# A decoder step on one core: two alternating buffers for the shared expert, and raw x turned with the norm's factors at the evictions

## The reference

```
h  = rmsnorm(x) * norm_mix_g;  z = h @ w_in          # q, k, v, o (512 each), gates i, f (4 each), u (512)
mix = [ mLSTM heads(q, k, v, i, f) * head_norm_g * sigmoid(o) | pooled(u) @ w_pool * pool_scale ]
x  = x + mix @ w_out
x  = x + shared_expert(rmsnorm(x)) + sum over top-8 of 64 experts: gate_e * (silu(h@w1_e) * (h@w3_e)) @ w2_e
x  = x + (p @ w_ple) * sigmoid(rmsnorm(x) @ w_gate);  y = rmsnorm(x) * final_norm_g
```

## Time and profile before

| | us |
|---|---|
| median of 3 runs | 1052.86 (1051.55 to 1054.36) |
| the profiled execution | 1053.18 |
| its span, first to last instruction | 1051.4 |
| start, until the gates (L1924) | 0 to 18.9 |
| projections, mixer, router, shared expert | 18.9 to 366 |
| expert loop | 366 to 956 |
| tail | 956 to 1051 |
| busy: PE, DVE, POOL, ACT | 985.3, 448.5, 360.4, 156.2 |

### The profile page before, as it was taken

The page is one execution under the profiler, slowest core; times in us unless marked ns, Lnnn a source line. Parts: engine busy times, 40 slices in busy tenths (PEclk is TensorE's granted clock), DMA queues, the critical chain, the costliest instruction groups (busy, mean ns, idle before and its releaser), DMA issues.

```text
span 1051.4 us, 16052 instructions
## 1 busy us (share of the span) xinstructions
PE 985.3 (94%) x5686; PEld 447.1 (43%) x5686; DVE 448.5 (43%) x1287; ACT 156.2 (15%) x383; POOL 360.4 (34%) x434
## 2 busy tenths in 40 slices
PE   5999999989999999999899899899899898999996
PEld 4777655645544433333233233233233233333443
DVE  4201222345549754344334344344333434452885
ACT  3110023301021101001011010001001001002322
POOL 5000321211024444444344344354344444451232
PEclk9999999999999999999999899899999999999999
DMA  9032223122149599999999999999999999796942
GB/s 295 20 92 80 81 78 90 54 67 70 41 147 386 192 371 400 413 413 413 411 396 413 405 394 412 403 390 413 390 394 402 387 402 397 283 366 257 422 159 80
DMA packets 76307, 296.43 MB, mean 282 GB/s; under 512 B 16250, under 2 KB 26682, under 8 KB 49381
## 3 DMA queue, kind: packets, MB, share of 16 engines
q1 hardware_dynamic: 59693, 258.14, 63.3%
q0 software_dynamic: 16576, 37.80, 9.4%
HBM read 277.08 MB, written 32.54 MB: 294 GB/s over the span
## 4 chain that ended last, share of the span: by engine, by line
PE 71%; DMA 14%; DVE 6%; issue 4%; POOL 2%; DVEq 1%; ACT 1%; SPq 0%; POOLq 0%; ACTq 0%
PE bank L1900 22%; PE bank L2270 19%; DMA xT<-in_ex_w 9%; PE bank L2249 6%; PE bank L2334 5%; PE bank L2252 5%; DMA arena<-xs_dram,slot 5%; PE bank L2273 4%; PE bank L1906 1%; POOL arena L919 1%; PE bank L1986 1%; PE bank L1996 1%; PE bank L2283 1%; PE bank L2033 1%; DVE arena L1816 1%
## 5 line engine op out<-in xcount | busy, mean ns | idle before, releaser
L2270 PE MATMUL bank<-arena 128*32 128x512 f32 x1536 | 240.3, 624 | 32.3 <-DMA xT<-in_ex_w 18.9
L919 POOL DMA_INDIRECT arena<-xs_dram,slot x200 | 220.8, 1104 | 71.1 <-issue 63.2
L2270 PE MATMUL bank<-xT,arena 128*32 128x512 f32 x512 | 239.8, 624 | 0.0
L2270 PEld LDWEIGHTS bank<-arena 128*32 128x32 f32 x1536 | 65.4, 114 | 179.8 <-issue 172.4
L934 POOL DMA_INDIRECT y_dram<-arena,outrow x48 | 49.1, 1024 | 267.7 <-DVE slot L1702 225.4
L2249 PE MATMUL bank<-arena 128*32 128x512 f32 x640 | 116.2, 595 | 0.8 <-ACT arena L1143 0.8
L1716 DVE STREAM_TRANSPOSE arena<-arena 128x1024 f32<-128x1024 f32 x50 | 62.2, 1243 | 86.7 <-DMA arena<-xs_dram,slot 86.7
L1900 PE MATMUL bank<-xT,ring 128*128 128x288 f32 x384 | 93.4, 406 | 0.0
L1900 PEld LDWEIGHTS bank<-xT,ring 128*128 128x128 f32 x384 | 72.9, 190 | 20.5 <-issue 0.5
L1139 ACT ACTIVATE arena<-bank 128x256 f32<-128x256 f32 x48 | 18.5, 385 | 358.9 <-PE bank L2270 253.0
L1764 DVE COPY outrow<-yrow 128x1 int32<-128x1 int32 x48 | 7.4, 154 | 144.2 <-PE bank L2249 94.5
(11 more groups left out here) (402 smaller groups left out, 1244.9 us busy)
## 6 DMA issues: line engine op xcount, KB each, us to landing
arena<-in_ex_w SPq DMA_DIRECT2D x96, 1024.0 KB, 15.2
ring<-in_ex_w SPq DMA_DIRECT2D x40, 1024.0 KB, 15.9
xT<-in_ex_w SPq DMA_DIRECT2D x32, 1024.0 KB, 10.4
arena<-y_dram SPq DMA_DIRECT2D x18, 1024.0 KB, 10.9
mixpj<-in_ex_w SPq DMA_DIRECT2D x16, 1024.0 KB, 12.3
ring<-in_w_in SPq DMA_DIRECT2D x5, 2048.0 KB, 8.3
wide<-in_ex_w SPq DMA_DIRECT2D x8, 1024.0 KB, 18.5
ring<-in_w_out SPq DMA_DIRECT2D x2, 2048.0 KB, 8.8
```

The lines of the kernel that those rows point to most:

```text
L919: pool.indirect_dma_start(xg[b][:, 256 * a:256 * a + 256], None, xs_quarter, bass.IndirectOffsetOnAxis(slot[k][:, a:a + 1], 0), bounds_che ...
L2270: ins = pe.matmul(bank[2][t, :], xgT[b][:, c, t], w13[k if lane < 3 else 3][:, :, wc, :], start=(c == 0), stop=(c == KT - 1))
```

## The change

Two edits in one. In the loop, own(j) becomes j % 3 and fourth(j) = 3 + j // 3 % 2 is new: the shared expert alternates between slots 3 and 4 and is loaded two periods ahead, the three own slots are refilled each period. SP's order and PE's waits follow. The last loads of SP are reordered: gt1, gt0, and then g_b, which now waits for the last w2 matmuls.

At the start PE turns x as it came. norm_mix_g is loaded with one value per partition and 128-row piece (g1) and multiplied in at the evictions of the turned tiles, all on DVE. POOL makes diag(rstd) for each tile; five matmuls of ones with it give rB, rstd along the free axis on all partitions, which ACT brings to SBUF. q and k (now evicted by DVE), u and the gates are multiplied by rB at their eviction, v and o by rstd as a value per partition (o's tanh takes rhalf = rstd / 2 as its scale). The gate biases are added after that, in two more passes.

```
-        g += [(("x1T", i, 0), "v"), (("x1T", i, 1), "s")]
-    g += [(("g",), "v")]
-    g += [(("q", j, n), "s") for j in range(H) for n in range(2)]
-    g += [(("k", j, n), "s") for j in range(H) for n in range(2)]
+        g += [(("x1T", i, 0), "v"), (("x1T", i, 1), "v")]
+    g += [(("rB", 0), "s"), (("rB", 1), "s"), (("g",), "v")]
+    g += [(("q", j, n), "v") for j in range(H) for n in range(2)]
+    g += [(("k", j, n), "v") for j in range(H) for n in range(2)]
...
-            return j % 3 or j // 3 % 2 * 4
+            return j % 3
+        def fourth(j):
+            return 3 + j // 3 % 2
...
-            sp.dma_start(g_a[:, :], bc(norm_mix_g[0])).then_inc(s_ga, 16)
+            sp.dma_start(g1, norm_mix_g[0].rearrange("(c p) -> p c", p=P),
+                         allow_slow_non_contiguous=True).then_inc(s_ga, 16)
...
-            e = expert(4)
+            e = expert(7)
...
+            def period(done, slot_c, place, last=None, more_c=True):
+                e = expert(place(0))
+                sp.wait_ge(s_mm1, done + 1)
+                load13(0, e)
                 if last is not None:
                     f = expert(last)
                     sp.wait_ge(s_mm2, done)
-                    load2(2, f)
+                    load2(7 - slot_c, f)
+                f, e = e, expert(place(1))
                 sp.wait_ge(s_mm1, done + 2)
                 load13(1, e)
+                sp.wait_ge(s_mm2, done + 1)
+                load2(0, f)
                 f, e = e, expert(place(2))
                 sp.wait_ge(s_mm1, done + 3)
                 load13(2, e)
+                sp.wait_ge(s_mm2, done + 2)
+                load2(1, f)
+                f = e
+                if more_c:
+                    e = expert(place(7))
+                    sp.wait_ge(s_mm1, done + 3)
+                    load13(slot_c, e)
                 sp.wait_ge(s_mm2, done + 3)
-                load2(3, f)
+                load2(2, f)
...
+            sp.wait_ge(s_mm1, more * STEPS + (STEPS - 2))
             load_chunk("gt1")
-            sp.wait_ge(s_mm2, more * STEPS + (STEPS - 2))
-            sp.dma_start(g_b[:, :], bc(final_norm_g)).then_inc(s_gb, 16)
             sp.wait_ge(s_mm2, more * STEPS + (STEPS - 1))
             load_chunk("gt0")
+            sp.wait_ge(s_mm2, more * STEPS + STEPS)
+            sp.dma_start(g_b[:, :], bc(final_norm_g)).then_inc(s_gb, 16)
...
             for i in range(NT):
+                r = ROWS[i]
                 rms(i, 0)
+                pool.wait_ge(s_rstd, i + 1)
+                pool.tensor_scalar(diag[0:r, i, 0:r], ident[0:r, 0:r], rstd[0:r, i:i + 1], None, ALU.mult
+                                   ).then_inc(s_diag, 1)
...
+            for i in range(NT):
+                r = ROWS[i]
+                for n in range(2):
+                    b = full_bank(dve, "x1T", i, n)
+                    drain("v", dve.tensor_tensor(
+                        xT[:, 4 * n:4 * n + 4, tok(i)], b[:, :].rearrange("p (c t) -> p c t", t=P)[:, :, 0:r],
+                        g1[:, 4 * n:4 * n + 4].unsqueeze(2).to_broadcast([P, 4, r]), ALU.mult), "x1T", i, n)
+
+            wait_drained(dve, "rB", 1)
+            dve.wait_ge(s_rstd, NT)
             b = full_bank(dve, "g")
...
+            for name, dst, scale in (("q", qT, float(P) ** -0.5), ("k", kT, 1.0)):
+                for j in range(H):
+                    for n in range(2):
+                        c = slice(TH * n, TH * n + TH)
+                        b = full_bank(dve, name, j, n)
+                        drain("v", dve.scalar_tensor_tensor(out=dst[:, j, c], in0=b[:, 0:TH], scalar=scale, in1=rB[:, c],
+                                                            op0=ALU.mult, op1=ALU.mult), name, j, n)
...
             for i in range(NT):
-                pe.wait_ge(s_xs, i + 1)
-                turn("x1T", i, xs1[:, i % 2, :])
+                pe.wait_ge(s_x[i], 16)
+                turn("x1T", i, x[:, i, :])
+            for n, tiles in enumerate((range(NP_), (NP_,))):
+                b = free_bank(pe, "rB", n)
+                for k, i in enumerate(tiles):
+                    r = ROWS[i]
+                    pe.wait_ge(s_diag, i + 1)
+                    ins = pe.matmul(b[:, P * k:P * k + r], onesf[0:r, :], diag[0:r, i, 0:r], start=True, stop=True)
+                ins.then_inc(filled, 1)
```

## The result

The changed kernel takes 1047.06 us (median of 5 runs, 1045.96 to 1048.96) against 1052.86: ratio 0.9944, interval 0.9930 to 0.9958. It is faster by 5.8 us, where 18.4 were forecast. The profiled execution has a span of 1047.2 us and a time of 1048.96.

The account below looks back on a forecast made before the run. The prediction took PE and DMA as both near full, the loop bound by DMA with stalls on the single shared buffer; 15.7 + 3.0 - 0.3 = 18.4 us off 1053.2 gave 1034.8, range 1028 to 1048.

Parts of the forecast that it names:

- The start: Before the gate matmuls: raw x turned, shorter path through rstd, gates begin at 15.9 instead of 18.91, 3.0 us gained.
- The tail: After the last w2 matmuls: g_b's load moved ahead of the y8 loads, taken as 0.3 us lost.
- term of 15.7 us: Expert loop, 420 to 930 us: its 202.2 MB at 409 GB/s take 494.3 us instead of 510, 15.7 gained.
- so this wait goes: Expert loop: two alternating shared buffers end PE's wait for the shared w1/w3 load, up to 19.1 us against a 15.3 gap.
- mean of 409 GB/s: Expert loop, 420 to 930 us: mean DMA rate taken to rise from 396.4 to 409 GB/s.
- 26.5 us, against up to 24.1 us to landing: Own experts' loads, the tightest left: freed at step j, wanted at j+3, 26.5 us later; landing takes up to 24.1.
- the wait only moves: Loop rival, 22%: stalls form on own experts' loads, the mean stays 399 GB/s, 6.3 us gained, 1047 us.
- 12.2 us a step from 12 to 42: Expert loop, sign to look for in the profile after: steps 12 to 42 at 12.2 us each, where before had 12.56.
- The slower rival: Loop rival, 8%: a deeper weight queue makes gathers land 1 us later, 12.8 us lost, 3.0 gained, 1063 us.
- the two bounds set: Gather pieces in the chain: under 9 us expected by the forecast; above 10 the slower rival holds.
- The 16 us: Loop gathers: called the slower rival's cost, to be 0 if DMA engines serve queue rows in turn.
- the second rival: Loop rival, 22%: the wait moves to own experts' loads; 3.3 us gained there plus 3.0 at the start, 1047 us.

Follow-up runs that it names:

- e_start: Start of the change alone (raw x turned, factors at the evictions), with the loop and tail of the kernel before: 1049.34 us, ratio to before 0.9960 to 0.9986.
- e_gb: Changed kernel with g_b's load issued behind the y8 loads and DVE's wait moved to its first use: 1045.91 us.
- e_order: Changed kernel with slot 0's next w1/w3 load issued by SP ahead of the previous period's slot 2 w2 load: 1044.49 us.
- e_bhalf: Kernel before, with only the first half of each w2 loaded and used twice: 1033.38 us.
- e_late: Changed kernel with SP's order and g_b's load mended (1042.5 us), plus the shared w1/w3 load issued one step later, behind slot 0's next: 1045.55 us.
- e_buffers: Buffers and tail of the change alone, with the start of the kernel before: 1049.97 us, ratio to before 0.9962 to 0.9987.

## Why the prediction was wrong, point by point

**The start** had the right path and about the right size, with some luck: 3.0 us forecast. In ten profiles with the new start the loop's first matmuls begin at 362.4 us on average, in three with the old one at 365.6, so 3.2. Only 2.5 of them are at the gates, where the path of the forecast ends: they begin at 16.25 on average for 18.77. The other 0.7 are the clock. From the gates to the loop it takes 346.8 to 347.0 us in six of the ten, with a granted clock of 0.83 from 210 to 220 us, and 345.1 to 345.3 in the four others, with 1.00; the three old ones, each with one such fall, took 346.8 to 347.0. Whether the change spares the fall in those four isn't shown. These are the windows of the changed kernel and of e_start, columns as in the earlier trace rows:

```profile
210.00:220.00 10.00, 7.98 (x32) 4.80 (x33) 4.72 (x9) 0.54 (x2) 1.87 (x1) 0.83 0.47 97
...
210.00:220.00 10.00, 7.97 (x36) 4.90 (x37) 4.72 (x9) 0.54 (x2) 1.87 (x1) 1.00 0.49 100
```

The timeline of the changed kernel, on PE and then POOL:

```profile
16.39 0.40 PE L1930 MATMUL bank<-arena,onesf 64*128 64x64 f32 x2 [0.76 <-POOL arena L756]
16.72 4.08 PE L1939 MATMUL bank<-xT,arena 128*36 128x288 f32 x32
20.73 3.66 PE L1908 MATMUL bank<-xT,ring 128*128 128x288 f32 x14
```

```profile
14.18 0.61 POOL L756 TENSOR_SCALAR arena<-ident,rstd 128x128 f32<-128x128 f32 x1
...
15.80 0.44 POOL L756 TENSOR_SCALAR arena<-ident,rstd 64x64 f32<-64x64 f32 x1
```

The gate matmuls (L1939, L1924 of before) start at 16.72 here and between 15.62 and 16.82 in the nine others, for 15.9 forecast. The path is the one named: the last tile's rstd, the diagonal, the small matmul. A whole diagonal costs 0.61, not the 0.41 of the earlier trace rows, and the last, half-sized one 0.44. q's chunk was not late: its matmuls start as the gates end. PE has no wait for the moved evictions in the profile.

**The tail** was mis-sized: 0.3 lost was forecast; 1.1 are by the medians (e_gb), and 1.4 to 4.1 by the profiles of the six kernels with this tail. The step that failed there is "DVE waits for it ahead of add_up(0), which itself needs the sum of those y8 rows, behind it in the same queue: hidden". It looked at who waits for g_b, and not at what the load runs beside: the last scatter, for which the y8 loads wait. Of the 4.1 in the changed kernel's profile that is 1.3; 1.7 are the clock's fall, and 0.8 lie before the scatter (18.4 us from step 47 to it, 17.6 in e_gb and e_order), unexplained.

**The loop** carried the error, and the step that failed is its term of 15.7 us, with "so this wait goes" and the mean of 409 GB/s that it rests on: 15.7 forecast, 5.6 measured (542.8 to 537.2; 4.8 as a mean of the first profiles of either loop). Three steps of it can be told apart.

First, the gap. "26.5 us, against up to 24.1 us to landing" took the slot's freeing for the issue. The issue comes 5.5 us later (691.93 to 697.38), so 21.0 were left. This was false, but it cost little: e_order mends it for 2.6 us at most.

Second, "so this wait goes; what is late next is the DMA rate itself" treated the stop as a property of the buffer. The runs show it as a property of the queue: with fewer bytes it goes even from the single buffer (e_bhalf), with an earlier issue it stays (e_order), and with another order it moves (e_late). A loop whose loads need 12.1 us a step beside 11.5 for PE must stop PE somewhere, and the engines run thin behind each stop. That was the reason given for the rival "the wait only moves"; it should have had the larger chance. The reason given against it, that more is issued behind such a stop, held for a small part: 5.6 of the 8.3 thin us remained.

Third, the rate. The 409 GB/s taken as the mean to come is about what the engines do when they are full, in every kernel with whole w1/w3 loads of 8 KB a partition and a rate in the table (408.9 to 411.5). As a mean it needs every thin window gone, those of 900 to 930 us too, where the last weights run out and no buffer helps. The 15.7 us are just that: 8.3 thin us up to 900, and some 7.5 in the 30 us at 307 GB/s. The change took 2.7 of the 8.3, and raised the end to 347, worth 2.9: 5.6. The single window of 426 and the stretch of 412 in the earlier trace rows lie above that mean and were taken for a level.

The forecast of 12.2 us a step from 12 to 42 was met with 12.25. It should have been a warning: 12.2 against 12.56 makes 10.8 us, so a third of the 15.7 had to come from the 14 other steps, for which the prediction names only the thin end (3.3). Measured are 9.4 us gained from 12 to 42, 1.0 from 42 to 47, and 4.8 lost from 3 to 12. The early loss needn't be a new cost. The changed kernel, e_buffers and e_gb took 110.3, 111.0 and 106.3 us from step 3 to 12, and yet 537.2, 537.4 and 537.8 from 3 to 47: in these three, PE that waited early waited less later.

**The slower rival** (gathers) didn't come. The longest gather of the changed kernel's chain took 9.49 us, between the two bounds set, others 8.38 and 7.39, beside 8.80 and 8.78 before. The 16 us that the prediction names as this rival's cost are in none of its sums; its own working gives 12.8. And the time, 1047.06, is that of the second rival, 1047, by its own mechanism in the loop. The exact match is luck: its 3.3 us there were too few and its tail cost nothing, and the two errors cancelled.

## What to carry to other kernels

Where a loop is near the DMA rate, measure the rate of full windows and the time lost in thin ones separately, and forecast from the second: in this kernel it was all that buffers or order could give back. A wait for a load in such a loop says which load was last in the queue, not which buffer is too few. A load that is moved costs what it runs beside, so look at the transfers of other queues in its new place.

## What the runs showed of the hardware

- 16 full DMA engines moved 408.9 to 411.5 GB/s of weights and gathers with w1/w3 loads of 8 KB a partition, and 398.1 and 399.9 with twice as many loads of 4 KB.
- A load issued 5 us sooner into a full queue landed no sooner (29.5 to 30.6 us after its issue, for 21.9 to 25.3).
- An indirect scatter of 128 rows took 5.27 to 5.47 us with a load of 0.5 MB beside it in six kernels, and 4.08 to 4.22 without it in six.
- With the same code in that stretch the granted clock fell to 0.50 in some profiles and not in others, behind a stretch in which PE was partly idle (busy 1.17 of 2 us and 2.14 of 4 us in the changed kernel): near 215 us in six of the ten with the new start, at the tail's first gate matmuls in four of the six with g_b in front. Each fall cost 1.7 us.
- The first matmuls of the loop, with the same start, came at 360.93 to 363.63 us in ten profiles, a spread of 2.7 us, as much as the start's part of this change is worth: 1.2 are from the gates' beginning, 1.7 from that fall of the clock.
